# Hybrid decoder trunk: the delta rule's sample rows and the order of the output projection's input

## The reference

```python
def step(s, xs):                      # delta rule; a sample row is one step from its own state s0
    q_i, k_i, u_i, w_i, g_i, a_i = xs
    v_new = u_i - jnp.einsum('bhcd,bhde->bhce', w_i, s)
    o_i = jnp.einsum('bhcd,bhde->bhce', q_i * jnp.exp(g_i)[..., None], s) + jnp.einsum('bhij,bhje->bhie', a_i, v_new)
    g_last = g_i[..., -1]
    s = s * jnp.exp(g_last)[..., None, None] + jnp.einsum(
        'bhcd,bhce->bhde', k_i * jnp.exp(g_last[..., None] - g_i)[..., None], v_new)
    return s, o_i
...
oa = (rmsnorm(oa, P['gnorm_a'][e]) * jax.nn.silu(za)).astype(h.dtype).reshape(B, L, W_V_A)
out = jnp.concatenate([oa, ob.reshape(B, L, W_B).astype(h.dtype)], axis=-1) @ P['w_out_e'][e]
...
x = x + cross_attn(rmsnorm(x, P['norm_x'][l]), mem_k[l], mem_v[l], l, P)
```

## Time and profile before

| | |
|---|---|
| runs, median (lowest to highest) | 4102.78 us (4101.08 to 4107.85) |
| profiled execution | 4096.77 us |
| its span, first to last instruction | 4095.2 us |
| PE busy | 3694.0 us (90%) |
| DVE, ACT, POOL busy | 39%, 17%, 32% |
| mean granted PE clock | 0.938 |

### The profile page before, as it was taken

One profiled execution on the slowest core, in us unless ns is written; L12 is line 12 of the kernel. 1 busy time (PEld: TensorE's weight loads), 2 busy tenths in 40 slices (PEclk: granted clock), 3 DMA queues, 4 the chain that ended last, 5 costly groups with the idle time before them and its releaser, 6 DMA issues.

```text
span 4095.2 us, 55933 instructions
## 1 busy us (share of the span) xinstructions
PE 3694.0 (90%) x22605; PEld 3392.7 (83%) x22605; DVE 1592.4 (39%) x1593; ACT 688.5 (17%) x1010; POOL 1302.2 (32%) x727
## 2 busy tenths in 40 slices
PE   5997899799969987899999998966997789999997
PEld 5766666688869876899999998926997689999997
DVE  1015659743243124331222235995305242223142
ACT  1014411122111122110100112103103121101010
POOL 1000013232212321344444444701141234444442
PEclk9899999799769998999999999987999899999998
DMA  1000135644221424111111111140232311111111
GB/s 75 31 21 0 42 109 173 130 130 127 90 96 62 145 72 160 36 47 46 47 46 47 46 46 44 62 104 26 84 118 92 144 36 46 46 47 46 47 47 57
DMA packets 82972, 293.96 MB, mean 72 GB/s; under 512 B 9753, under 2 KB 10026, under 8 KB 79378
## 3 DMA queue, kind: packets, MB, share of 16 engines
q1 hardware_dynamic: 58466, 181.24, 14.5%
q0 software_dynamic: 24368, 110.67, 8.0%
HBM read 265.98 MB, written 26.94 MB: 72 GB/s over the span
## 4 chain that ended last, share of the span: by engine, by line
PE 71%; DVE 11%; issue 10%; ACT 3%; DMA 2%; POOL 2%; DVEq 0%; POOLq 0%; SPq 0%; ACTq 0%
PE ps L525 48%; PE ps L514 3%; PE ps L591 2%; DVE wk L1021 1%; PE ps L1320 1%; PE ps L1626 1%; PE ps L726 1%; PE ps L1313 1%; PE ps L1322 1%; PE ps L1280 1%; PE ps L745 1%; DMA w_raw<-wallb 1%; DVE wk L1023 1%; PE ps L1631 1%; PE ps L1694 1%
## 5 line engine op out<-in xcount | busy, mean ns | idle before, releaser
L293 POOL TENSOR_TENSOR w_hi<-w_raw,ones 128x1024 fp32r<-128x1024 f32 x192 | 466.1, 2427 | 1194.9 <-PE ps L525 1153.9
L525 PE MATMUL ps<-h_hi,w_hi 128*128 128x344 f32 x3072 | 663.5, 325 | 62.1 <-DVE h_lo L487 33.8
L525 PE MATMUL ps<-h_lo,w_hi 128*128 128x344 f32 x3072 | 659.0, 323 | 0.0
L525 PE MATMUL ps<-h_hi,w_lo 128*128 128x344 f32 x3072 | 655.0, 322 | 0.0
L525 PEld LDWEIGHTS ps<-h_hi,w_hi 128*128 128x128 f32 x3072 | 523.5, 191 | 68.4 <-issue 40.6
L294 POOL TENSOR_TENSOR w_lo<-w_raw,w_hi 128x1024 fp32r<-128x1024 f32 x192 | 555.8, 2895 | 15.1
L525 PEld LDWEIGHTS ps<-h_lo,w_hi 128*128 128x128 f32 x3072 | 526.6, 191 | 0.0
L525 PEld LDWEIGHTS ps<-h_hi,w_lo 128*128 128x128 f32 x3072 | 518.4, 190 | 0.0
L514 PE MATMUL ps<-hT,w 128*128 128x344 f32 x1152 | 340.3, 458 | 4.7 <-ACT wk L1081 2.0
L525 PE MATMUL ps<-a_lo,w_hi 128*128 128x344 f32 x1536 | 325.9, 320 | 0.0
L525 PE MATMUL ps<-a_hi,w_hi 128*128 128x344 f32 x1536 | 325.8, 320 | 0.0
(11 more groups left out here) (422 smaller groups left out, 4123.6 us busy)
## 6 DMA issues: line engine op xcount, KB each, us to landing
w_raw<-wallb SPq DMA_DIRECT2D x224, 512.0 KB, 3.5
xT<-kpool POOLq DMA_DIRECT2D x128, 256.0 KB, 3.2
xT<-vpool SPq DMA_DIRECT2D x128, 256.0 KB, 2.9
xT<-cmk POOLq DMA_DIRECT2D x16, 1024.0 KB, 5.4
w<-wall SPq DMA_DIRECT2D x14, 1024.0 KB, 5.1
x<-x_spill SPq DMA_DIRECT2D x32, 270.0 KB, 12.3
x_spill<-xT POOLq DMA_DIRECT2D x2, 4128.0 KB, 19.8
xT<-x_spill POOLq DMA_DIRECT2D x2, 4128.0 KB, 13.9
```

The source lines that it names most:

```text
L293: S["pool"].link(nc.gpsimd.tensor_tensor(w_hi[:, s], w_raw[:, s], one, ALU.mult))
L525: ins = nc.tensor.matmul(ps[:, 3 * (j % 2) + n, 0:N3], wt[:, j % 2, k, :], src[:, k, n * N3:(n + 1) * N3], start=(k == 0 and n_pass == 0), ...
```

## The change

- The factors of the sample rows are spread at the start of the delta rule: DVE builds one 128 × 352 product (`dve_row_factors`), PE spreads it in one matmul (`pe_row_factors`), and DVE makes the scaled q, k, v there. L1482 and its 24 matmuls go.
- The states come into the start of `xT` as soon as the last page has been used. They are only read from there.
- Spreading of the new values and the state updates leave this place. The states are loaded a second time, in four parts, into free memory behind the first split, and PE spreads eight values (`pe_row_values`) behind each of the projection's tiles 4 to 7 into banks 6 and 7; DVE updates eight states (`dve_row_states`) behind the residual of the same tile. The four stores follow between the memory stage's keys and values.
- `act_cat` and `dve_cat` come in two halves: chunks 4 to 7 (attention) right behind the delta rule, chunks 0 to 3 behind the head norm. The projection takes its chunks in that order. The head norm uses banks 3, 4, 6, 7 for the prompt and 5 for the samples.
- The first two weight splits wait for the new values, no longer for the end of the head norm.

```diff
@@ -466,6 +466,8 @@
                 nc.vector.tensor_tensor(acc, acc, sq[:, c % 2], ALU.add).then_inc(nm_add, 1)
+                if l == 0 and c >= 4:
+                    dve_row_states(dve, c - 4)
                 if c == 1:
@@ -515,16 +517,16 @@
-        def product3_tile(pe, j, hi, lo, wait_src=None):
-
-            for k in range(KC):
+        def product3_tile(pe, j, hi, lo, wait_src=None, chunks=range(KC)):
+
+            for k in chunks:
                 if wait_src is not None:
...
                         ins = nc.tensor.matmul(ps[:, 3 * (j % 2) + n, 0:N3], wt[:, j % 2, k, :],
-                                               src[:, k, n * N3:(n + 1) * N3], start=(k == 0 and n_pass == 0),
-                                               stop=(k == KC - 1 and n_pass == 2))
+                                               src[:, k, n * N3:(n + 1) * N3], start=(k == chunks[0] and n_pass == 0),
+                                               stop=(k == chunks[-1] and n_pass == 2))
             ins.then_inc(psum_ready, 1)
@@ -546,7 +548,11 @@
                 pe.wait_ge(psum_free, g0 + j - 1)
-                product3_tile(pe, j, hi, lo, wait_src if j == 0 else None)
+                if name == "out" and j == 1:
+                    pe.wait_ge(gn["u"], HA + 1)
+                product3_tile(pe, j, hi, lo, wait_src if j == 0 else None, CAT if name == "out" else range(KC))
+                if name == "out" and j >= 4:
+                    pe_row_values(pe, j - 4)
@@ -1115,7 +1121,8 @@
+        gtf = gt[:, :, :, :].rearrange("p t k h -> p (t k h)")
+        l_st, l_rc = part(gtf, 96, 72), part(gtf, 168, 72)
@@ -1284,6 +1291,7 @@
                 spread(group)
+            pe_row_factors(pe)
             for r in range(ROUNDS):
@@ -1415,6 +1423,7 @@
                 take(group)
+            dve_row_factors(dve)
             for r in range(ROUNDS):
@@ -1459,98 +1468,142 @@
+        gs = {n: sem("gs_" + n) for n in ("st", "cb", "ps", "vn", "vr", "out")}
         NS = HA * NB
...
+        st_in = part(xTf, 0, NB, HA, P)
+        st_q = [part(la, 5120 + 1024 * q, 8, P) for q in range(3)] + [part(masks, 0, 8, P)]
+        g_rows = part(wk, 2048, 11 * HA, NB)
+        g_cb = part(wk, 7932, 11, HA, NB)
+        r_k, r_el, r_vn = (part(gtf, 32 * n, HA, NB) for n in range(3))
...
         def pool_gdn_rows(pool):
+            pool.wait_ge(fs["free"], 66)
+            pool.dma_start(st_in.rearrange("p b h n -> p (b h) n"), st_gdn.rearrange("b h p n -> p (b h) n"))\
+                .then_inc(gs["st"], 16)
             pool.wait_ge(gd["s"], QT + 1)
             store(pool, gdn_p, S_)
...
+            pool.wait_ge(gs["vn"], 2)
             pool.wait_ge(fs["out"], 2)
...
+        def pool_row_states(pool):
+            for q in range(4):
+                pool.dma_start(st_q[q], st_gdn[2 * q:2 * q + 2].rearrange("b h p n -> p (b h) n")).then_inc(gs["st"], 16)
...
+        def pool_keep_states(pool):
+            pool.wait_ge(gs["out"], 4)
+            for q in range(4):
+                store(pool, gdn_s[:, 8 * q:8 * q + 8], st_q[q])
+            kept["states"] = 16 * n_stored[0]
...
+        def pe_row_factors(pe):
...
+            pe.wait_ge(gs["cb"], 1)
+            nc.tensor.matmul(ps[:, 7, 0:352], ones[:], g_rows.rearrange("p k b -> p (k b)"), start=True, stop=True)\
+                .then_inc(gs["ps"], 1)
...
         def pe_gdn_rows(pe):
...
             pe.wait_ge(gs["st"], 16)
...
+            pe.wait_ge(gs["cb"], 2)
+            pe.wait_ge(fs["pvc"], 2 * ROUNDS)
             for h in range(HA):
                 for b in range(NB):
...
+                    nc.tensor.matmul(ps[:, 6, 2 * (h * NB + b):2 * (h * NB + b) + 2], st_in[:, b, h, :], g_pair[:, h, b, :],
                                      start=True, stop=True)
...
                 .then_inc(gs["ps"], 1)
...
+        def pe_row_values(pe, q):
...
+            pe.wait_ge(gs["vn"], 2)
+            pe.wait_ge(nm_cp, M_NORM[0] + 1)
+            if q:
+                pe.wait_ge(gs["out"], q)
+            for n in range(8):
+                b, h = 2 * q + n // HA, n % HA
+                ins = nc.tensor.matmul(psf[:, 3072 + n * P:3072 + (n + 1) * P], r_vn[:, h, b:b + 1].to_broadcast([P, P]),
+                                       ident[:], start=True, stop=True)
             ins.then_inc(gs["vr"], 1)
...
+        def dve_row_factors(dve):
+            link, vv = S["dve"].link, nc.vector
+            vv.tensor_tensor(g_rows, gt[:, QT, :, :].rearrange("p k (h b) -> p (k h) b", b=1).to_broadcast([P, 11 * HA, NB]),
+                             ident[:, P - NB:P].rearrange("p (a b) -> p a b", a=1).to_broadcast([P, 11 * HA, NB]), ALU.mult)\
+                .then_inc(gs["cb"], 1)
+            dve.wait_ge(gs["ps"], 1)
+            link(vv.tensor_copy(g_cb.rearrange("p k h b -> p (k h b)"), ps[:, 7, 0:352]))
...
+            vv.tensor_tensor(g_qk, g_q, g_k, ALU.mult).then_inc(gs["cb"], 1)
...
             link, vv = S["dve"].link, nc.vector
...
+            dve.wait_ge(gs["ps"], 2)
             vv.tensor_tensor(cols[:, 8:12], g_qk, pr[:, :, :, 1], ALU.add).then_inc(gs["vn"], 1)
...
+            vv.tensor_copy(r_k, g_k)
+            vv.tensor_copy(r_el, g_cb[:, G_EL])
+            vv.tensor_copy(r_vn, g_vn).then_inc(gs["vn"], 1)
...
+        def dve_row_states(dve, q):
...
+            vv = nc.vector
+            if q == 0:
+                dve.wait_ge(gs["st"], 80)
+                dve.wait_ge(gs["vn"], 2)
+            dve.wait_ge(gs["vr"], q + 1)
             lag = S["dve"].lag
...
+            def decay(n):
...
+                return vv.tensor_scalar(st_q[q][:, n, :], st_q[q][:, n, :], r_el[:, h, b:b + 1], None, ALU.mult)
...
+            def update(n):
...
+                return vv.scalar_tensor_tensor(out=st_q[q][:, n, :], in0=psf[:, 3072 + n * P:3072 + (n + 1) * P],
+                                               scalar=r_k[:, h, b:b + 1], in1=st_q[q][:, n, :], op0=ALU.mult, op1=ALU.add)
...
             lag(decay(0))
...
+            for n in range(1, 8):
+                lag(decay(n))
+                lag(update(n - 1))
+            S["dve"].link(update(7))
             dve.sem_inc(gs["out"], 1)
...
         gn = {n: sem("gn_" + n) for n in ("rc", "bc", "u")}
...
+        n_t = part(bigf, 6160, 2, T)
+        o_sq = part(bigf, 4096, 2, T)
...
+        n_s = part(bigf, 8224, HA, NB)
...
         def pe_head_norm(pe):
...
+            pe.wait_ge(gs["vn"], 1)
+            pe.wait_ge(gd["oc"], QT)
+            pe_squares(pe, 8, HA, o_sq)
             pe.wait_ge(gn["rc"], 1)
             for h in range(HA):
+                nc.tensor.matmul(ps[:, 5, h * NB:(h + 1) * NB], l_rc[:, h * 9 + QT:h * 9 + QT + 1].to_broadcast([P, P]),
+                                 ident[:, P - NB:P], start=True, stop=True)
+            for h in range(HA):
                 if h >= 2:
...
+                    pe.wait_ge(gn["u"], h)
+                base = (1536, 3072)[h % 2]
+                for t in range(QT):
+                    ins = nc.tensor.matmul(psf[:, base + t * P:base + (t + 1) * P],
+                                           l_rc[:, h * 9 + t:h * 9 + t + 1].to_broadcast([P, P]), ident[:],
                                            start=True, stop=True)
@@ -1558,13 +1611,16 @@
             vv.reciprocal(l_rc[:, 0:36], l_st[:, 0:36]).then_inc(gn["rc"], 1)
+            dve.wait_ge(gn["bc"], 1)
+            link(vv.scalar_tensor_tensor(out=n_s, in0=big[:, 8:12, SEQ:T], scalar=v("gnorm"),
+                                         in1=ps[:, 5, 0:NS].rearrange("p (h b) -> p h b", b=NB), op0=ALU.mult, op1=ALU.mult))
+            vv.tensor_tensor(aT[:, 0:HA, SEQ:T], aT[:, 0:HA, SEQ:T], n_s, ALU.mult).then_inc(gn["u"], 1)
             for h in range(HA):
                 dve.wait_ge(gn["bc"], h + 1)
-                if h >= 2:
-                    dve.wait_ge(gn["u"], h - 1)
...
-                vv.tensor_tensor(aT[:, h, :], aT[:, h, :], n_t[:, h % 2], ALU.mult).then_inc(gn["u"], 1)
+                base = (1536, 3072)[h % 2]
...
+                vv.tensor_tensor(aT[:, h, 0:SEQ], aT[:, h, 0:SEQ], n_t[:, h % 2, 0:SEQ], ALU.mult).then_inc(gn["u"], 1)
@@ -1594,16 +1650,22 @@
-        cat_hi, cat_lo, mix_free = sem("cat_hi"), sem("cat_lo"), sem("mix_free")
-
-        def act_cat(act):
-            act.wait_ge(mix_free, 1)
-            for c in range(KC):
+        cat_hi, cat_lo, states_kept = sem("cat_hi"), sem("cat_lo"), sem("states_kept")
+        CAT = [4, 5, 6, 7, 0, 1, 2, 3]
+
+        def act_cat(act, half):
+            if half == 0:
+                act.wait_ge(fs["out"], 2)
+                act.wait_ge(gd["oc"], QT)
+            else:
+                act.wait_ge(gn["u"], HA + 1)
+            for c in CAT[4 * half:4 * half + 4]:
                 nc.scalar.activation(h_hi[:, c, :], aT[:, c, :], ACT.Copy).then_inc(cat_hi, 1)
-        def dve_cat(dve):
-            for c in range(KC):
-                dve.wait_ge(cat_hi, c + 1)
+        def dve_cat(dve, half):
```

(27 more changed lines are left out.)

69 lines of the change are left out of this document (13 added, 56 removed).

## The result

| kernel | median us (lowest to highest, runs) | kernel before, same chip | ratio, 95% interval |
|---|---|---|---|
| changed | 4052.64 (4042.14 to 4057.40, 4) | 4101.93 | 0.9874, 0.9852 to 0.9896 |
| changed, again (after_again) | 4054.25 (4043.37 to 4063.81, 5) | 4098.44 | 0.9893, 0.9875 to 0.9911 |
| before, again (before_again) | 4101.02 (4094.72 to 4107.42, 11) | 4098.44 | 1.0007, 0.9998 to 1.0016 |

The account below looks back on a forecast made before the run. A chain of waits, one engine at a time, was taken to bound the kernel. 50.9 ahead less 7.1 for row values and 3 for stores gave 40.8: 4056.0 profiled, with 6 to the median 4062.0, range 4053 to 4080.

Parts of the forecast that it names:

- Factors, 1.1: Front of the delta rule: one more DVE product and one 352-column matmul add 1.1 us to the path, between 0 and 3.
- Reads, 9.5: Behind the delta rule: the 64 reads of the sample states, 45 at full clock and 19 at half, take 9.5 us.
- Rival B: Early states do not come early, landing near 1132; reads then run at half clock, time 4078.3; chance 0.06.
- Squares 39.1 earlier: Head norm's squares begin at 1132.0, 39.1 us ahead, with row values and state updates gone from between reads and squares.
- Tile 0's residual 50.9 ahead: Output projection: tile 0 ends at 1172.1, where its residual began at 1223.01 before, 50.9 us ahead.
- Row values 7.1, updates and memory rows 0: Output projection: broadcasts behind tiles 4 to 7 cost 7.1 us; state updates and later-landing memory rows cost nothing.
- Stores 3: Memory stage: four state stores beside the weight tile loads cost 3 us, between bounds 0 and 6.5.
- A: Memory stage: stores hold up a weight tile as x_spill did, memory rows come 4 late; 12.7 more, 4074.7; chance 0.14.
- rival C: Output projection stays at clock 0.50 because of row values between tiles and split tile 0; time 4140; chance 0.03.
- The sum: Whole kernel: 50.9 - 7.1 - 3 = 40.8 us gained, so the profiled execution would take 4056.0.
- The rule on turns between queues: DMA engines alternate between queues with work, so a load beside one stream takes about twice its time, 7.0 us.

Follow-up runs that it names:

- late_factors_cut: Changed kernel ended behind the first memory stage, with the row factors made behind the delta rule as before; 1341.49 to 1359.71 us, median 1346.55.
- after_cut: Changed kernel ended behind the first memory stage, otherwise unaltered; 1327.69 to 1341.88 us, the kernel before so ended 1376.45 to 1378.43.
- after_delay2_cut: Changed kernel ended behind the first memory stage, with two idle matmuls ahead of the delta rule's first round; 1326.68, 1328.66, 1330.05, 1338.46, 1340.78 us.
- before_delay_cut: Kernel before, ended behind the first memory stage, with four idle matmuls ahead of the delta rule's first round; 1366.47 to 1381.58 us.
- after_fill_cut: Changed kernel ended behind the first memory stage, with four idle matmuls in each step's gap in the delta rule's last round; 1319.93 to 1329.12 us.

## Why the prediction was right, and where it failed

- **Factors, 1.1:** the rounds start 0.7 later in the profile (11.1 from the first spread to the first product, 10.4 before), 1.3 to 1.9 in the five others, and 1.1 between late_factors_cut and after_cut. Right in size. That something so small ahead of the last round can be worth 12 us in it was not seen.
- **Reads, 9.5:** 9.14 (8.65 and 0.49), the states in time, the clock 0.80; 8.95 to 11.99 in the five others, depending on when the clock fell. Rival B falls.
- **Squares 39.1 earlier:** 38.1, counted from the rule's first spread (816.1 before, 818.7 after; the program up to there is not changed); 33.8 to 39.5 in the five others.
- **Tile 0's residual 50.9 ahead:** 49.3, counted likewise. The half, the updates and the factors put back one at a time were worth 7, 24 and 8 on the path; the early states were not put back alone.
- **Row values 7.1, updates and memory rows 0:** four pieces of 1.78 are 7.1, and tile 3 follows tile 2 with only its sums between them. Right.
- **Stores 3:** some 4 by the length of the memory stage. The `w_raw` tile loaded beside them landed after 6.82 to 7.51 in the six profiles, not after x_spill's 15.2, so A falls. That the clock falls behind so long a wait (1.5 to 1.6 in five of six) was not in the term.
- **Clock of the projection (rival C):** 1.00 throughout. Falls there.
- **The sum:** 4056.0 for the profiled execution, 4057.4 measured. In part this is luck: the mean of the six is 4059.9, 38.7 below the two profiles of the kernel before (4096.77 and 4100.43), where the sum said 40.8. (3 MB at x_spill's rate are 15.3 us and not 15.4, which changes nothing.)

The rule on turns between queues (the Trainium skill, DMA: Bandwidth & Descriptors, "Queues, rings and completion order") gave 7.0 for a load beside one stream. The loads beside the stores took 6.82 to 7.51, so here the trace agrees; why the one beside x_spill took 15.2 stays open.

**The step that failed** is the last one, from the profile to the median. I added 6 us because the profile of the kernel before lay that much under its median, and took 3 us for the spread of runs from the same kernel. Both carry over only if the change leaves alone how the executions differ. It did not: the median lies 4.8 *below* the profile of the changed kernel, and 1.4 + (-6) + (-4.8) = -9.4 is the whole miss of 4052.6 against 4062.0, 0.4 below the range. The 6 was one draw even for the kernel before: in before_again the profile lies 0.6 under the median (4100.43 and 4101.02). What the runs showed in its place is a stage with two values that no step of mine priced, the delta rule's last round. In part of the executions, two of five in after_cut, it holds full clock for 44 us and not 28, and the rule is 12 us shorter. Long executions follow the sum within 4 us (4059.9 against 4056.0), some 40 below the medians of before; the short ones pull the median down.

**What is shown and what is not.** Shown: the spread arises ahead of the queries (after_cut), the last round is 12.1 shorter in a profile of the short kind (after_delay2_cut), a delay at the rule's front alone produces a spread like it (before_delay_cut, with the reserve above), and work in the last round's gaps alone, which keeps its clock up, takes the long executions away (after_fill_cut). Not shown: that it is the factors, and not another part of the change, that let short executions appear; and the short kind in a profile of the unaltered changed kernel; all six, and that of after_cut, were long, and there it is read from times and mean clocks. Whether profiled executions are less often of the short kind can't be told from so few. Behind the first cross scores the profiles differ by up to 7 us (2615.1 to 2618.7 us to the end in the six of the changed kernel, 2618.8 and 2622.0 before); which stage does that was not followed up.

The Trainium skill (TensorE: Matmul & The Clock Gate, "A second HAM failure mode: psum-queue depth-cycling") tells of a kernel whose small pauses between groups of matmuls made it go back and forth between the clocks. I had weighed it for the projection, where the trace does not show it; in the rule's last round the clock falls once and comes back once, with pauses of 0.69 us, and filling them was worth 18.7 us of that round.

## What to carry to other kernels

Before a sum is carried from a profile to a median, look for long stretches at half clock in stages that a change merely shifts: a microsecond of delay ahead of one can go with executions ten shorter (before_delay_cut), and a single profile then shows one kind of execution only. Ending both kernels behind the stage in question turns a spread of 20 us in 4000 into one that can be read (2 against 14). The mean clock of each run helps to tell the kinds apart (0.921 to 0.926 and 0.935 to 0.937 in after_cut), but not always: in after_delay2_cut it was 0.928 for 1330.05 and 0.927 for 1338.46. Where TensorE waits in short gaps inside dense work, it is worth trying to fill them with idle matmuls: with the earlier stores this took another 13 to 15 us off the median (4039.56 against 4052.64 and 4054.25, on different chips).

## What was not expected of the hardware

- A delay of about 0.9 us on TensorE made whole executions up to 10 us shorter (1366.47 against 1376.45 to 1378.43, on different chips).
- With gaps of 0.69 us between groups of 56 matmul instructions the clock fell to 0.50 after 27 to 30 us in one execution and after 44 in another of nearly the same program; with the gaps filled it stayed at 1.00 for 66.7.
- The reads, 32 products of 2 columns (64 instructions) behind work at 1.00, kept that clock for 4.4 us or more and lost it while TensorE was busy (0.51 in the next stretch).
